# Sixteen of 22 contraction tiles of a last projection put through Strassen's method

## The chip, the cores and the metric

The kernel runs on one core of a Trainium2 chip. The metric is the device time of one execution in microseconds; the median of three runs of the kernel before is 2008.83 us (2007.9 to 2009.86). Times called "at 1873.53" are microseconds from the start of the profiled execution's span.

## The reference

Two layers of a streaming encoder on x of 1 x 512 x 1024 (float32). Each layer is a half-step SwiGLU FFN, a mixer (gated DeltaNet heads and a convolution module) and a second half-step FFN, each between two RMSNorms, then a block norm. The change touches only the last product of the second layer's second FFN and what follows it:

```python
def swiglu_ffn(x, w_in, w_out):        # D_MODEL 1024, D_FF 2816
    h = x @ w_in
    gate, up = h[..., :D_FF], h[..., D_FF:]
    return (jax.nn.silu(gate) * up) @ w_out
...
    h = swiglu_ffn(rms_norm(x, ffn2_norm_pre[l]), ffn2_w_in[l], ffn2_w_out[l])
    x = x + 0.5 * rms_norm(h, ffn2_norm_post[l])
    x = rms_norm(x, block_norm[l])
```

## The kernel before

Every large product is computed to nearly full float32 precision from three products of rounded float32r operands: high by high, high by low and low by high, where high is the rounded tensor (ScalarE, ACT, makes it) and low is the exact tensor minus high (VectorE, DVE, makes it). Weights come by DMA into four slots `raw` (512 KB each, the SP queue issues them), ACT writes `wh`, DVE writes `wl`, and TensorE (PE) takes both. Semaphores count the units: `lo_full` after each `wl`, `unit_done` when PE has used a slot.

An FFN computes 22 tiles (128 rows) of h. Tiles 5 to 20 (`CONV0`, `NS` = 16) already go through a seven-product Strassen scheme in the FFN's first product, one tile per `body`, on all three engines in software-pipelined order; the tiles 0 to 4 and 21 are plain pairs of `in_unit`. After the last `body`, PE runs `in_unit` for the gate half of tile 21, two remaining products (`p4`, `p3`) and `in_unit` for its up half. Meanwhile ACT (`h_high`, `h_rounded`) and DVE (`h_low`) split the 16 exact tiles `hraw` into `hh` and `hl`, two at a time; DVE also finishes the tiles 20 and 21 (lines 2406 to 2431).

For the last FFN of the last layer PE then runs `rows_out` (line 831). Here h is the stationary operand (128 contraction rows by 128 tokens) and the weights stream past in 512 columns, so the output has tokens on partitions. The output is 4 token chunks `c` by 2 column halves, and its eight 128x512 accumulators fill the eight PSUM banks (`row_banks`). For each of 22 contraction tiles k there are 4 chunks x 3 products x 2 halves = 24 matmuls (`row_tile`, line 816). The first 18 tiles go k by k over all chunks. The last four (`HELD`) stay in the four slots and are taken chunk by chunk, so that chunk 0 is complete first and its tail runs beside the matmuls of chunks 1 to 3.

The weights of a tile are one DMA of 512 KB (line 510), one ACT copy of 128x1024 (line 1356, `high`) and one DVE subtraction of 128x1024 (line 2074, `weight_low`), with four slots in flight. The two gain rows (`grow`) are loaded in the middle.

The tail of a chunk (lines 1973 to 2022 on ACT, 2817 to 2892 on DVE): ACT squares the two halves out of PSUM and sums them, DVE multiplies the same banks by the gain into `yrow` and adds the residual row (turned by PE's `turn_row` into the freed banks), ACT squares that, DVE scales it twice into `xin`, and SP stores it. The order of each engine is written out by hand: ACT `row_root(0)`, `row_root(1)`, `block_root(0)`, `row_root(2)`, `block_root(1)`, `last_square(0)`, `block_root(2)`, `last_square(1)`; DVE `row_gained`, `row_factor`, `row_added`, `row_scaled` likewise. An engine never passes a waiting instruction. `steps.link(x)` on DVE issues x and waits for its completion.

Of the kernel before, what the change touches and what calls it, by code (L numbers as in the profile page):

```python
# [46 lines left out]
def trunk_kernel(nc, x, ffn1_norm_pre, ffn1_w_in, ffn1_w_out, ffn1_norm_post, mix_norm_pre, mix_w_in,  # L47
# [103 lines left out]
    T2_, T3_, T1_, T4_ = range(4)  # L151
    ring = at("ring", [P, 2, SLOTS * 8 * P], F32, o_wh)
# [99 lines left out]
    with ctx:  # L252
# [89 lines left out]
        conv_hi, conv_lo, conv_done = [sem(n) for n in ("conv_hi", "conv_lo", "conv_done")]  # L342
        rows_done, R_DONE = s_xturn, KD
# [75 lines left out]

        HELD = 4  # L420
# [31 lines left out]
        def _(sp):  # L452
# [13 lines left out]
            for l in range(L):  # L466
                def ffn(f):
# [39 lines left out]
                    if f == 1 and l == L - 1:  # L507
                        for k in range(KF):
                            sp.wait_ge(lo_full, l * UNITS + UBASE[f] + IN_U + k + 1)
                            sp.dma_start(raw[:, k % SLOTS, :, :].rearrange("p a b -> p (a b)"),  # L510
                                         ffn2_w_out[l, k * P:(k + 1) * P, :]).then_inc(raw_full[k % SLOTS], 16)
                            if k == KF // 2:

                                sp.wait_ge(h_ready, L * NP)
# [31 lines left out]
            for c in range(NC):  # L546
                for half in range(2):
# [5 lines left out]
                    sp.dma_start(out[0, c * P:(c + 1) * P, cols], xin[:, c, cols]).then_inc(s_out, 16)  # L553
# [62 lines left out]
        def _(pe):  # L616
# [199 lines left out]
            def row_tile(c, k, halves=(0, 1)):  # L816
                tokens = slice(c * P, (c + 1) * P)
                for j, (h, w) in enumerate(((hh, wh), (hh, wl), (hl, wh))):
                    for half in halves:
                        mm = pe.matmul(row_banks(c)[:, half, :], h[:, k, tokens],  # L820
                                       w[:, k % SLOTS, 4 * half:4 * half + 4, :].rearrange("p a b -> p (a b)"),
                                       start=k == 0 and j == 0, stop=k == KF - 1 and j == 2)
                return mm
# [7 lines left out]
            def rows_out(u1):  # L831
                at0 = (L - 1) * UNITS + u1 + SLOTS
                pe.wait_ge(pair_free, (L - 1) * NP + 2 * KF - 1)
                pe.wait_ge(c12_out, 2 * L * NS + 2)
                for k in range(KF - HELD):
                    if k in range(CONV0, CONV0 + NS, 2):
                        pe.wait_ge(conv_done, (2 * L - 1) * NCONV + (k - CONV0) // 2 + 1)
                    pe.wait_ge(lo_full, at0 + k + 1)
                    pe.wait_ge(h_ready, (L - 1) * NP + KF + k + 1)
                    for c in range(NC):  # L840
                        if k == 0 and c >= 2:
                            pe.wait_ge(pair_free, (L - 1) * NP + 2 * KF - 3 + c)
                        mm = row_tile(c, k)
                    mm.then_inc(unit_done, 1)
                for c in range(NC - 1):
                    for k in range(KF - HELD, KF):
                        if c == 0 and k in range(CONV0, CONV0 + NS, 2):
                            pe.wait_ge(conv_done, (2 * L - 1) * NCONV + (k - CONV0) // 2 + 1)
                        if c == 0:
                            pe.wait_ge(lo_full, at0 + k + 1)  # L850
                            pe.wait_ge(h_ready, (L - 1) * NP + KF + k + 1)
                        mm = row_tile(c, k)
                    mm.then_inc(rows_done, 1)
                    if c in (1, 2):

                        pe.wait_ge(rows_sq, R_SQ + 2 * c)
                        pe.wait_ge(rows_gained, R_GAINED + 2 * c)
                        turn_row(c - 1, row_banks(c - 1))
                for half in range(2):
                    for k in range(KF - HELD, KF):  # L860
                        mm = row_tile(NC - 1, k, (half,))
                    mm.then_inc(rows_done, 1)
                    if half == 0:
                        pe.wait_ge(rows_sq, R_SQ + 2 * 3)
                        pe.wait_ge(rows_gained, R_GAINED + 2 * 3)
# [485 lines left out]
        def _(act):  # L1351
# [93 lines left out]
            def ffn(f, l):  # L1445
# [100 lines left out]
                def body(s, odd, first=False, final=False):  # L1546
# [16 lines left out]
                    if final:  # L1563
                        act.wait_ge(prod_done, st * PRODS + 7 * s + 6)
                        high(u0 + 2 * (KF - 1) + 1, 3, 8, l)
                        h_high(0)
                        h_high(1)
# [21 lines left out]
                def out_high(v):  # L1589
                    high(u0 + IN_U + v, v, 8 if last else part[v % 3], l)  # L1590
# [29 lines left out]
                body(NS - 1, 0, final=True)  # L1620
                h_rounded(0)
# [22 lines left out]
                if last:  # L1644
                    for k in range(SLOTS, KF):
                        high(u0 + IN_U + k, k % SLOTS, 8, l)
                    return
# [52 lines left out]
            for l in range(L):  # L1700
# [271 lines left out]
                ffn(1, l)  # L1972
            def row_root(c):
                act.wait_ge(rows_done, R_DONE + c + 1)
                for half in range(2):
                    if half:
                        act.wait_ge(rows_gained, R_GAINED + 2 * c + 1)
                    act.activation(spare[:, half * T:(half + 1) * T], row_banks(c)[:, half, :], ACT.Square,
                                   accum_out=yss[:, c, half:half + 1]).then_inc(rows_sq, 1)
# [12 lines left out]
            def last_square(half):  # L1992
                act.wait_ge(rows_done, R_DONE + NC + half)
                act.activation(spare[:, half * T:(half + 1) * T], row_banks(3)[:, half, :], ACT.Square,
                               accum_out=yss[:, 3, half:half + 1]).then_inc(rows_sq, 1)
# [26 lines left out]
            act.activation(xin[:, 3, T:D], xin[:, 3, T:D], ACT.Copy, scale=xrec[:, 3:4]).then_inc(row_out_last, 1)  # L2022
# [3 lines left out]
        def _(dve):  # L2026
# [186 lines left out]
            def ffn(f, l):  # L2213
# [116 lines left out]
                def body(s, odd, made=True, first=False, final=False):  # L2330
# [16 lines left out]
                    if final:  # L2347
                        weight_low(u0 + 2 * (KF - 1) + 1, 3, 8, l)
                        h_low(0)
                        h_low(1)  # L2350
# [9 lines left out]
                def out_low(v):  # L2360
                    weight_low(u0 + IN_U + v, v, 8 if last else part[v % 3], l)
# [44 lines left out]
                ps = pair_steps()  # L2406
                up_second(LAST_S, 0)
# [8 lines left out]
                p = KF - 1  # L2416
                dve.wait_ge(unit_done, l * UNITS + u0 + 2 * p + SLOTS + 1)
                dve.tensor_tensor(gs[:, 1, :], in_bank(unit_bank(6, stage, l)), rs[:], ALU.mult).then_inc(gate_scaled, 1)
                h_low(4)
                dve.wait_ge(unit_done, l * UNITS + u0 + 2 * p + SLOTS + 2)  # L2420
                dve.tensor_tensor(us[:, 1, :], in_bank(unit_bank(7, stage, l)), rs[:], ALU.mult).then_inc(pair_free, 1)
                dve.wait_ge(pair_free, l * NP + f * KF + p + 1)
                dve.wait_ge(silu_done, l * NP + f * KF + p + 1)
                ps.link(dve.tensor_tensor(hf[:], gs[:, 1, :], us[:, 1, :], ALU.mult))
                ps.link(dve.tensor_scalar(hh[:, p, :], hf[:], 1.0, None, ALU.mult))
                dve.tensor_tensor(hl[:, p, :], hf[:], hh[:, p, :].bitcast(F32), ALU.subtract).then_inc(h_ready, 1)
# [5 lines left out]
                if last:  # L2432
                    for k in range(SLOTS, KF):
                        weight_low(u0 + IN_U + k, k % SLOTS, 8, l)
                    return
# [380 lines left out]

            def row_gained(c):
                dve.wait_ge(rows_done, R_DONE + c + 1)
                for half in (1, 0):
                    if half == 0:  # L2820
                        dve.wait_ge(rows_sq, R_SQ + 2 * c + 1)
# [96 lines left out]
```

## Time and profile before

| | |
|---|---|
| median of 3 runs | 2008.83 us |
| profiled execution, first to last instruction | 2007.0 us |
| PE busy | 1958.0 us (98%), 12162 matmuls |
| DVE busy, ACT busy | 1440.1 us (72%), 1140.7 us (57%) |
| `rows_out` on PE | from 1873.53 to 1996.8 us, 528 matmuls of 128x512 |
| tail after the last matmul | to 2007.0 us |

The profiled execution lasts 2007.0 us by its span; the runs' median is 1.8 us more. Busy time counts the instructions of an engine; a matmul's end is modelled, so the time from one start to the next (the pitch) says more than the mean duration. A timeline row gives start, duration, engine, line, operation, output<-inputs, shape, and in brackets an idle time before it with what ended it. "x2" merges equal neighbours: their time runs from the first start to the last end.

### The profile page before, as it was taken

Reading aid. Unit: us, or ns where it says so; the run is one execution under the profiler, and the core shown is the slowest. Engines: PE = TensorE matmul, PEld = TensorE weight load, DVE = VectorE, ACT = ScalarE, POOL = GpSimd, SP = SyncE. Lnnn points to the kernel's source line nnn. Section 1 sums busy time; section 2 is a strip of 40 time slices with the busy share of each in tenths; the row PEclk is TensorE's granted clock in tenths of the full one; section 3 lists DMA queues with packets and bytes.
Section 4 is the critical chain, followed back from the end, with each engine's and each line's share of the span. In section 5 each row is a group of like instructions: output and inputs, shape, how many; then the busy total and the mean of one; then the engine's idle time right before and its main releaser. Section 6 shows DMA issues by size and latency. Waiting matters only on the chain.

```text
span 2007.0 us, 33275 instructions
## 1 busy us (share of the span) xinstructions
PE 1958.0 (98%) x12162; PEld 1751.0 (87%) x12162; DVE 1440.1 (72%) x2129; ACT 1140.7 (57%) x1915; POOL 149.2 (7%) x196
## 2 busy tenths in 40 slices
PE   9999999999999999999999999999999999999997
PEld 7899988878988799988878999888879887999886
DVE  5988832699785888872388888337997868888524
ACT  6566742457765566662365667325586655666623
POOL 1111000011000011100001110000110000111000
PEclk9999999999999999999999999999999999999999
DMA  6466533376222366643315664433761223666421
GB/s 174 104 156 156 145 106 100 79 163 139 61 53 84 84 146 151 157 125 99 98 53 127 157 157 130 116 101 77 171 147 27 64 74 90 161 156 149 158 95 42
DMA packets 351424, 232.49 MB, mean 116 GB/s; under 512 B 11123, under 2 KB 324949, under 8 KB 351317
## 3 DMA queue, kind: packets, MB, share of 16 engines
q1 hardware_dynamic: 327396, 177.55, 30.9%
q0 software_dynamic: 23904, 53.49, 14.9%
q8 instruction: 70, 1.15, 0.2%
q14 instruction: 38, 0.30, 0.0%
q10 hardware_dynamic: 16, 0.00, 0.0%
HBM read 175.43 MB, written 2.10 MB: 88 GB/s over the span
## 4 chain that ended last, share of the span: by engine, by line
PE 72%; DVE 16%; ACT 7%; issue 4%; DMA 1%; POOL 0%; SPq 0%; DVEq 0%; ACTq 0%
PE res L654 9%; PE res L655 9%; PE res L656 9%; PE res L889 7%; PE res L891 7%; PE res L892 7%; DVE u L2491 4%; PE sp L820 3%; PE sp L889 3%; PE sp L891 3%; PE sp L892 3%; PE res L820 2%; DVE cacc L2573 2%; PE sp L1132 1%; PE sp L1141 1%
## 5 line engine op out<-in xcount | busy, mean ns | idle before, releaser
L2074 DVE TENSOR_TENSOR wl<-raw,wh 128x1024 fp32r<-128x1024 f32 (+1 forms) x167 | 197.3, 1185 | 336.4 <-ACT wh L1356 335.9
L1356 ACT ACTIVATE wh<-raw 128x1024 fp32r<-128x1024 f32 (+1 forms) x205 | 209.7, 1029 | 332.0 <-PE res L656 238.0
L654 PE MATMUL res<-xh,wh 128*128 128x512 f32 x536 | 214.8, 401 | 10.7 <-DVE wl L2074 6.5
L889 PE MATMUL res<-xh,wh 128*128 128x256 f32 x768 | 218.6, 285 | 4.3 <-DMA wl<-raw 2.8
L891 PE MATMUL res<-xl,wh 128*128 128x256 f32 x768 | 217.7, 283 | 0.0
L892 PE MATMUL res<-xh,wl 128*128 128x256 f32 x768 | 217.6, 283 | 0.0
L656 PE MATMUL res<-xh,wl 128*128 128x512 f32 x536 | 210.0, 392 | 0.0
L655 PE MATMUL res<-xl,wh 128*128 128x512 f32 x536 | 209.7, 391 | 0.0
L656 PE MATMUL res<-hh,wl 128*128 128x512 f32 (+1 forms) x528 | 198.7, 376 | 0.0
L654 PE MATMUL res<-hh,wh 128*128 128x512 f32 (+1 forms) x528 | 198.7, 376 | 0.0
L655 PE MATMUL res<-hl,wh 128*128 128x512 f32 (+1 forms) x528 | 198.7, 376 | 0.0
L602 POOL DMA_DIRECT2D wl<-raw x128 | 108.9, 855 | 1012.2 <-ACT wl L1497 998.9
L2491 DVE SCALAR_TENSOR_TENSOR u<-glu,call,u 128x512 f32<-128x512 f32 x240 | 167.8, 746 | 0.3
L889 PEld LDWEIGHTS res<-xh,wh 128*128 128x128 f32 x768 | 147.5, 192 | 6.3 <-ACT wh L1507 3.1
L889 PE MATMUL res<-th,wh 128*128 128x256 f32 x512 | 145.7, 285 | 5.0 <-DVE wl L2277 2.6
L891 PEld LDWEIGHTS res<-xl,wh 128*128 128x128 f32 x768 | 147.5, 192 | 0.2
L892 PEld LDWEIGHTS res<-xh,wl 128*128 128x128 f32 x768 | 147.5, 192 | 0.0
L889 PE MATMUL sp<-th,wh 128*128 128x256 f32 x512 | 145.3, 284 | 1.8 <-DVE us L2300 1.8
L891 PE MATMUL sp<-tl,wh 128*128 128x256 f32 x512 | 145.2, 284 | 0.0
L892 PE MATMUL sp<-th,wl 128*128 128x256 f32 x512 | 145.1, 283 | 0.0
L891 PE MATMUL res<-tl,wh 128*128 128x256 f32 x512 | 145.1, 283 | 0.0
L892 PE MATMUL res<-th,wl 128*128 128x256 f32 x512 | 145.1, 283 | 0.0
(419 smaller groups left out, 4884.2 us busy)
## 6 DMA issues: line engine op xcount, KB each, us to landing
raw<-in_ffn_w_in SPq DMA_DIRECT2D x176, 512.0 KB, 4.1
wl<-raw POOLq DMA_DIRECT2D x128, 256.0 KB, 5.3
raw<-in_mix_w_in SPq DMA_DIRECT2D x48, 512.0 KB, 4.0
raw<-in_ffn_w_out SPq DMA_DIRECT2D x46, 512.0 KB, 4.0
raw<-in_ffn_w_out SPq DMA_DIRECT2D x48, 448.0 KB, 3.8
wl<-raw POOLq DMA_DIRECT2D x38, 512.0 KB, 5.0
raw<-in_mix_w_out SPq DMA_DIRECT2D x16, 512.0 KB, 4.2
xin<-in_x SPq DMA_DIRECT2D x8, 256.0 KB, 5.9
```

Of the source, the lines that this page charges most:

```text
L602: pool.dma_start(wl[:, 2, ks, :].bitcast(F32), raw[:, 2 * ((SP0 + s) % 2), ks, :], accum_op=ALU.add).then_inc(form_added[half], 16)
L654: pe.matmul(bank, wh[:, slot, j, :], hi, start=first, stop=False)
L655: pe.matmul(bank, wh[:, slot, j, :], lo, start=False, stop=False)
L656: return pe.matmul(bank, wl[:, slot, j, :], hi, start=False, stop=last)
L820: mm = pe.matmul(row_banks(c)[:, half, :], h[:, k, tokens], w[:, k % SLOTS, 4 * half:4 * half + 4, :].rearrange("p a b -> p (a b)"), start ...
L889: pe.matmul(bank, wh[:, slot, j, :], hi[:, k, :], start=first and k == 0, stop=False, skip_group_check=True)
L891: pe.matmul(bank, wh[:, slot, j, :], lo[:, k, :], start=False, stop=False, skip_group_check=True)
L892: mm = pe.matmul(bank, wl[:, slot, j, :], hi[:, k, :], start=False, stop=k == 3, skip_group_check=True)
L1356: act.activation(wh[:, slot, 0:nk, :], raw[:, slot, 0:nk, :], ACT.Copy).then_inc(hi_full, 1)
L2074: dve.tensor_tensor(wl[:, slot, 0:nk, :], raw[:, slot, 0:nk, :], wh[:, slot, 0:nk, :].bitcast(F32), ALU.subtract).then_inc(lo_full, 1)
L2491: ins = dve.scalar_tensor_tensor(u[:, t, :], src, w, u[:, t, :], ALU.mult, ALU.add)
L2573: ins = dve.scalar_tensor_tensor(cacc[:, n % 2, :], pre[:, k:k + T], w, cacc[:, n % 2, :], ALU.mult, ALU.add)
```

## The change

The contraction tiles 5 to 20 are taken in eight pairs j: tile 5+j (`SUMMED`) and tile 13+j (`DIRECT`). With tokens halved (256 each) and output columns halved (512 each), each pair is a 2x2 block product, done by the seven-product form of Strassen's method. A product is 2 token chunks x 3 = 6 matmuls of 128x512. Four products per pair come in a first pass over j (S3*T3, S2*T2, S1*T1 and A11*B11), three in a second (A22, S4 and A12 with their weights), and the six plain tiles follow, the last four of them chunk by chunk as before. The banks c22, c21, c12 accumulate one product each over the first pass; these and c11 are then copied out (`alone`, eight ACT copies of 128x512), the second pass accumulates on in c21, c12 and c11, and six DVE additions (`make_addends`) make the three sums that each chunk's tail adds to its banks (`row_sum`).

Removed: `h_high`, `h_low`, `h_rounded` and the weight splits of this stage. The other three FFN outputs stay as they are. Operand work, first pass, per pair j: DVE forms S1, S2, S3, S4 (four subtractions or additions of 128x256), the weight sums (three of 128x512), the low parts of h (128x768 and 128x256) and of the weights (1024, 512, 512). ACT makes the matching high parts. Second pass, per pair: DVE one weight sum of 512, low parts 1024 and 512, and 512 and 256 of h. Weight slots are used in pairs, so two sets of operands are in flight. `h_last` is the finish of tile 21 (lines 2422 to 2426), `up_last` line 2421.

```diff
 # PE, rows_out (rows_product: 2 token chunks x 3 matmuls of 128x512)
-                for k in range(KF - HELD):
-                    ...
-                        mm = row_tile(c, k)
-                    mm.then_inc(unit_done, 1)
+                for j in range(NJ):
+                    q = j % 2
+                    pe.wait_ge(a_low, W0 + j + 1)
+                    pe.wait_ge(w_low, W0 + j + 1)
+                    mm7 = rows_product(j, q, F_S3, 4 + F_S3, 3, c22, j == 0)
+                    mm6 = rows_product(j, q, F_S2, 4 + F_S2, 2, c21, j == 0)
+                    if j == 0:
+                        pe.wait_ge(pair_free, (L - 1) * NP + 2 * KF)
+                    mm5 = rows_product(j, q, F_S1, 4 + F_S1, 0, c12, j == 0)
+                    ...
+                    rows_product(j, q, F_A11, 4 + F_A11, 1, c11, j == 0).then_inc(rows_unit, 1)
+                for j in range(NJ):
+                    ...
+                    rows_product(j, q, F_A22, 4 + F_A22, 2, c21)
+                    rows_product(j, q, F_S4, F_S4 + 1, 0, c12)
+                    rows_product(j, q, F_A12, 4 + F_A12, 1, c11).then_inc(rows_unit, 1)
+                n = len(PLAIN) - HELD
+                for i in range(n):
+                    pe.wait_ge(w_low, W0 + 2 * NJ + i + 1)
+                    ...
 # SP: 512 KB of the summed tile, 256 KB of the direct one, then 512 KB of the direct one again
+                                if j < 2:
+                                    sp.wait_ge(lo_full, l * UNITS + UBASE[f] + IN_U + 2 * j + n + 1)
+                                else:
+                                    sp.wait_ge(w_low, W0 + j - 1)
+                                load_row(2 * (j % 2) + n, k, cols)
 # ACT
+                def forms_high(j):
+                    act.wait_ge(a_sum, W0 + j + 1)
+                    act.activation(h_cells(j, 1, 3), h_cells(j, 5, 3, False), ACT.Copy)
+                    act.activation(h_cells(j, 0), hraw[:, SUMMED[j], SECOND_T], ACT.Copy).then_inc(a_high, 1)
+                def sums_high(j):
+                    ...
+                        act.wait_ge(rows_unit, W0 + j - 1)
+                    act.wait_ge(w_sum, W0 + j + 1)
+                    act.activation(w[:, 0:2 * T], r[:, 0:2 * T], ACT.Copy).then_inc(w_high, 1)
+                    act.activation(w[:, 3 * T:4 * T], r[:, 3 * T:4 * T], ACT.Copy).then_inc(w_high, 1)
+                    act.activation(w[:, 2 * T:3 * T], kept_sums[j][:], ACT.Copy).then_inc(w_high, 1)
 # DVE
+                def form_sums_of_h(j, steps):
+                    ...
+                    at_s1 = steps.done(dve.tensor_tensor(s1, a21, a22, ALU.add))
+                    dve.tensor_tensor(s3, a11, a21, ALU.subtract)
+                    steps.need(at_s1)
+                    steps.link(dve.tensor_tensor(s2, s1, a11, ALU.subtract))
+                    dve.tensor_tensor(a21, a12, s2, ALU.subtract).then_inc(a_sum, 1)
+                def weight_sums(j, steps):
+                    ...
+                    dve.tensor_tensor(t3, b22, b12, ALU.subtract)
+                    steps.link(dve.tensor_tensor(b12, b12, b11, ALU.subtract))
+                    dve.tensor_tensor(kept_sums[j][:], b22, b12, ALU.subtract).then_inc(w_sum, 1)
+                if last:
+                    up_second(LAST_S, 0)
+                    h_made(LAST_S - 1, 1)
+                    form_sums_of_h(1, ps)
+                    up_first(LAST_S, 0, ps)
+                    weight_sums(0, ps)
+                    forms_low(0)
+                    gate_times(LAST_S, 0)
+                    weights_low(0)
+                    forms_low(1)
+                    h_made(LAST_S, 0)
+                    form_sums_of_h(2, ps)
+                    form_sums_of_h(3, ps)
+                    gate_last()
+                    weight_sums(1, ps)
+                    forms_low(2)
+                    up_last()
+                    forms_low(3)
+                    weights_low(1)
+                    h_last()
+                    for j in range(2, NJ):
+                        if j + 2 < NJ:
+                            form_sums_of_h(j + 2, ps)
+                        weight_sums(j, ps)
+                        if j + 2 < NJ:
+                            forms_low(j + 2)
+                        weights_low(j)
+                        if j >= 6:
+                            later_forms_low(j - 6)
+                    ...
+                    for j in range(1, NJ):
+                        later_weight_sum(j)
+                        later_weights_low(j)
+                        if j + 1 < NJ:
+                            later_forms_low(j + 1)
+                    dve.wait_ge(a_low, W0 + 2 * NJ)
+                    make_addends(ps)
+                    for i in range(len(PLAIN)):
+                        plain_low(i)
+                    return
 # tail, DVE: row_sum before row_gain; chunks 0 and 1 sum both halves, 2 and 3 the first
+            def row_sum(c, half):
+                n = (0, 1)[half] if c < 2 else 2
+                dve.tensor_tensor(yrow[:, c, half * T:(half + 1) * T], row_banks(c)[:, half, :], addends[:, n, c % 2, :],
+                                  ALU.add).then_inc(row_summed, 1)
 # tail, ACT: the square of a summed half waits for row_sum
+            def row_square(c, half):
+                if c >= 2 and half == 1:
+                    src = row_banks(c)[:, half, :]
+                else:
+                    act.wait_ge(row_summed, W0 + (2 * c + half if c < 2 else c + 2) + 1)
```

## Rows read from the trace of the kernel before

**Rows 1.** Groups of instructions of the output stage, 1861 to 1997 us.

```profile
L820 PE MATMUL res<-wh,hh 128*128 128x512 f32 x88 | 28.1, 393 | 0.0
L2074 DVE TENSOR_TENSOR wl<-raw,wh 128x1024 fp32r<-128x1024 f32 x23 | 28.0, 1224 | 68.2 <-ACT wh L1356 68.2
L1356 ACT ACTIVATE wh<-raw 128x1024 fp32r<-128x1024 f32 x22 | 23.0, 1057 | 67.9 <-PE res L820 67.9
```

**Rows 2.** The chain that ended last, one of its steps (start, us, count).

```profile
1911.77 2.72 PE sp L820 x12
```

**Rows 3.** Timeline of DVE before and at the hand-over, 1843 to 1880 us.

```profile
1844.82 0.69 DVE L2267 TENSOR_TENSOR ring<-raw 128x512 f32<-128x512 f32 x1
1845.55 0.69 DVE L2268 TENSOR_TENSOR raw<-raw 128x512 f32<-128x512 f32 x1
...
1850.78 0.41 DVE L2300 TENSOR_TENSOR us<-us,res 128x256 f32<-128x256 f32 x1
1851.11 0.68 DVE L2328 TENSOR_TENSOR hraw<-gs,us 128x512 f32<-128x512 f32 x1
1851.71 0.69 DVE L2284 TENSOR_TENSOR wl<-raw,wh 128x512 fp32r<-128x512 f32 x1
...
1861.17 2.35 DVE L2357 TENSOR_TENSOR hl<-hraw,hl 128x1024 fp32r<-128x1024 f32 x2
...
1866.83 0.42 DVE L2313 TENSOR_TENSOR us<-us,sp 128x256 f32<-128x256 f32 x1 [1.13 <-PE sp L892]
1867.28 0.69 DVE L2317 TENSOR_TENSOR us<-us,rs 128x512 f32<-128x512 f32 x1
```

**Rows 4.** Timeline of ACT, the same stretch.

```profile
1843.13 0.62 ACT L1497 ACTIVATE wl<-raw 128x512 fp32r<-128x512 f32 x1
1843.65 0.62 ACT L1498 ACTIVATE wh<-raw 128x512 fp32r<-128x512 f32 x1
...
1859.53 2.00 ACT L1583 ACTIVATE hl<-hraw 128x1024 fp32r<-128x1024 f32 x2
...
1868.74 0.36 ACT L1544 ACTIVATE gs<-res 128x256 f32<-128x256 f32 x1
```

**Rows 5.** Timeline of PE at the end of the first product.

```profile
1873.31 0.39 PE L656 MATMUL res<-xh,wl 128*128 128x512 f32 x1
1873.53 0.62 PE L820 MATMUL sp<-wh,hh 128*128 128x512 f32 x2
```

**Rows 6.** DMA issues, 1850 to 1990 us: count, size, median us to landing.

```profile
raw<-in_ffn_w_out SPq DMA_DIRECT2D x22, 512.0 KB, 3.5
```

**Rows 7.** Timeline of the tail, 1976 to 2008 us.

```profile
1988.94 0.68 DVE L2825 TENSOR_TENSOR yrow<-res,grow 128x512 f32<-128x512 f32 x1
...
1995.26 1.28 DVE L2836 SCALAR_TENSOR_TENSOR xrow<-yrow,yrec,res 128x1024 f32<-128x1024 f32 x1
...
1996.63 1.06 ACT L1987 ACTIVATE spare<-xrow 128x1024 f32<-128x1024 f32 x1 [2.36 <-DVE xrow L2836]
...
2003.38 0.72 ACT L2022 ACTIVATE xin<-xin,xrec 128x512 f32<-128x512 f32 x1 [0.32 <-DVE xrec L2889]
```

**Rows 8.** Timeline of PE around its longest wait.

```profile
1050.58 0.39 PE L656 MATMUL res<-xh,wl 128*128 128x512 f32 x1
1054.08 0.47 PE L654 MATMUL res<-xh,wh 128*128 128x512 f32 x1 [3.12 <-DVE wl L2074]
...
1055.08 0.63 PE L654 MATMUL res<-xh,wh 128*128 128x512 f32 x1
1055.50 0.63 PE L655 MATMUL res<-xl,wh 128*128 128x512 f32 x1
...
1058.27 0.40 PE L656 MATMUL res<-xh,wl 128*128 128x512 f32 x1
```

**Rows 9.** Engine busy by stretch: length, PE, PEld, DVE, ACT, POOL, granted clock, DMA share, GB/s.

```profile
1056.00:1058.00 2.00, 2.00 (x6) 1.59 (x5) 2.00 (x3) 0.00 (x0) 0.00 (x0) 0.50 0.58 174
...
1873.53:1960.60 87.07, 87.07 (x386) 72.14 (x385) 27.82 (x26) 26.45 (x27) 0.00 (x0) 1.00 0.35 118
```

More of the change, by code:

```diff
@@ L1620, in ffn @@
                 body(NS - 1, 0, final=True)
+                if last:
+                    forms_high(1)
+                    gate_second(LAST_S, 0)
+                    sums_high(0)
+                    silu(KF - 2, 0)
+                    forms_high(2)
+                    forms_high(3)
+                    silu(KF - 1, 1)
+                    sums_high(1)
+                    act.activation(warm[:], eps[:], ACT.Sqrt)
+                    for j in range(2, NJ):
+                        if j + 2 < NJ:
+                            forms_high(j + 2)
+                        sums_high(j)
+                        if j >= 6:
+                            later_forms_high(j - 6)
+                    later_sums_high(0)
+                    for n in range(8):
+                        alone(n)
+                    for j in range(1, NJ):
+                        later_sums_high(j)
+                        if j + 1 < NJ:
+                            later_forms_high(j + 1)
+                    for i in range(len(PLAIN)):
+                        plain_high(i)
+                    return
                 h_rounded(0)
@@ L2348, in body @@
                         weight_low(u0 + 2 * (KF - 1) + 1, 3, 8, l)
-                        h_low(0)
-                        h_low(1)
+                        if last:
+                            form_sums_of_h(0, ps)
+                        else:
+                            h_low(0)
+                            h_low(1)
                     else:
@@ new lines, in plain_low, with make_addends @@
+                def plain_low(i):
+                    dve.wait_ge(w_high, W0 + 5 * NJ + i + 1)
+                    dve.tensor_tensor(wl[:, i % SLOTS], raw[:, i % SLOTS], wh[:, i % SLOTS].bitcast(F32),
+                                      ALU.subtract).then_inc(w_low, 1)
+                def make_addends(steps):
+                    dve.wait_ge(alone_out, W0 + 8)
+                    p7, p6, p5, p1 = [[h_cells(2 * n + t, 2, 2, False) for t in range(2)] for n in range(4)]
+                    for t in range(2):
+                        steps.link(dve.tensor_tensor(addends[:, 2, t, :], p1[t], p6[t], ALU.add))
+                        dve.tensor_tensor(addends[:, 1, t, :], p1[t], p7[t], ALU.add)
+                        steps.link(dve.tensor_tensor(addends[:, 0, t, :], addends[:, 2, t, :], p5[t], ALU.add))
@@ L2415, in ffn @@
                 h_made(LAST_S, 0)
-                p = KF - 1
-                dve.wait_ge(unit_done, l * UNITS + u0 + 2 * p + SLOTS + 1)
-                dve.tensor_tensor(gs[:, 1, :], in_bank(unit_bank(6, stage, l)), rs[:], ALU.mult).then_inc(gate_scaled, 1)
+                gate_last()
                 h_low(4)
[L2420 to L2426, printed above, removed]
+                up_last()
+                h_last()
                 out_low(2)
```

307 lines of the change are left out of this document (238 added, 69 removed).

## The prediction

> **What bounds the kernel now.** The page first: PE is busy 98% of the span, DVE 72%, ACT 57%, so in general a matmul saved is time saved. That average is of no use for one stage, so the second view is busy time by stretch. Over the first sixteen contraction tiles of the output PE is busy all 87.07 us at the full clock, DVE only 27.8 and ACT 26.5 [rows 9]. The groups of this stage agree: DVE's weight splits wait 68.2 us for ACT, whose copies wait 67.9 us for PE to free a slot, and PE waits for nothing [rows 1]. The chain of waits runs through PE in steps of twelve matmuls, 2.72 us each, a pitch of 0.2267 us [rows 2]. So PE sets the end here, and DVE has about 59 us to spare in 87. The question is what the change asks of DVE, and when.
>
> **Fewer matmuls.** Before: six groups of 88 like the first of [rows 1], 528. After: 8 pairs x 7 products x 6 = 336, and 6 plain tiles x 24 = 144, 480 in all, of the same shape and kind. 48 x 0.2267 = **10.9 us saved**. One pair is 24 matmuls = 5.44 us in the first pass, 18 = 4.08 us in the second; a plain tile is 5.44 us as before.
>
> **DVE's prices.** From start to next start [rows 3]: 128x512 0.60 us, 128x256 0.33, 128x1024 1.13 (2.35 less one duration of 1.22), and 768 between these, 0.86 (estimated from its neighbours). Where the instruction's own end is awaited: 512 0.73 (1844.82 to 1845.55), 256 0.45 (1866.83 to 1867.28). ACT [rows 4]: 1024 0.95, 512 0.52, 768 about 0.74, 256 about 0.3.
>
> **The first pass on DVE.** Sums of h 0.33 + 0.33 + 0.45 + 0.33 = 1.45; weight sums 0.60 + 0.73 + 0.60 = 1.93; low parts of h 0.86 + 0.33 = 1.20; low parts of weights 1.13 + 0.60 + 0.60 = 2.33. Together **6.9 us per pair, against PE's 5.44**. ACT needs 1.1 + 2.0 us per pair, in the shadow of DVE's next piece. So DVE is the bound of this pass for pairs 2 to 5, and PE idles 1.5 us per pair. Two operand sets in flight shift that, they don't remove it.
>
> **The hand-over**, followed in DVE's written order from 1861.2, where the first `h_low` starts now [rows 3]. Sums of pair 0 to 1862.6, `up_second` to 1863.0; ACT can make `forms_high(0)` only after the sums, which puts its silu behind them, to 1864.4, and `h_made` to 1864.5; sums of pair 1 to 1866.6; `up_first` waits for PE as now (1866.83) and ends 1868.0; weight sums 0 to 1869.9; low h 0 to 1871.1; `gate_times` 1871.7; low weights 0 done at 1874.1. PE wants them at 1873.5 [rows 5]: idle 0.6. Then come low h 1, `h_made`, sums 2 and 3, `gate_last`, weight sums 1, low h 2 and `up_last` (1.2 + 0.6 + 1.45 + 1.45 + 0.6 + 1.93 + 1.2 + 0.7 = 9.1), done at 1883.2. PE needs that `up_last` before its third product of pair 0, since c12 lies in the bank it reads: it arrives at 1874.2 + 12 x 0.2267 = 1876.9 and **waits 6.3 us**. Behind `up_last` on DVE stand low h 3 and low weights 1, done 1886.7 (PE idle 0.8), then `h_last` (0.73 + 0.47 + 0.6) and a full pair of 6.9: weights 2 done 1895.4 (PE idle 3.3). Pairs 3, 4 and 5 follow each 6.9 later (idle 3 x 1.5). Pairs 6 and 7 have no sums of h, but then nothing covers ACT's 1.05 us between weight sums and low weights: 5.4, and 6.3 for pair 7 with `later_forms_low(0)` (idle 0.1 and 1.0). The pass ends at 1933.7.
>
> **The second pass** costs DVE 0.60 + 1.13 + 0.60 + 0.60 + 0.33 = 3.3 us per pair and ACT 2.3, against 4.08 on PE. A slot pair freed by PE is filled again 2.9 us later (0.95 ACT, then 1.13 and 0.69 DVE), so PE stays busy but for 0.2. The copies `alone` (8 x 0.52 on ACT) are each ready before their bank's second product. `make_addends`, 4 linked x 0.73 + 2 x 0.60 = 4.1 us, stands before the first `plain_low`; the tile is ready 0.3 us late. Plain tiles cost DVE and ACT 2.1 us of 5.44, as now.
>
> Idle in all: 0.6 + 6.3 + 0.8 + 3.3 + 4.5 + 0.1 + 1.0 + 0.2 + 0.3 = **17.1 us against 10.9 saved, so PE ends 6.2 us later**.
>
> **The loads.** A pair brings 768 KB per 6.9 us = 114 GB/s, the stretch now runs at 118 [rows 9]. A load of 512 KB lands 3.5 us after its issue [rows 6]; those of pairs 2 to 5 are issued at least 8 us before use, those of pair 7 some 7 us before (issued 1916, wanted 1923). Nothing is added; one late landing there would cost 1 us.
>
> **The tail.** I followed the order of the three engines with the durations of [rows 7]; for the kernel before the same sums end at 2004.1, as the trace does (2003.38 + 0.72). `row_sum` reads a PSUM bank like the gain product does, 0.6 to 0.69 us [rows 7]. Two per chunk in chunks 0 and 1, one in 2 and 3. DVE's slack swallows part, and the residual add of chunk 2 (1995.26) comes 1.4 us later. Then ACT's `last_square(0)`, which before found its bank long ready, stands ahead of `block_root(2)` (1996.63) and waits for DVE's new `row_sum` of chunk 3: 0.6 + 0.6 more. All that follows to the last instruction moves: **+2.6 us**. Bounds: 0 if the queue hides it, 6 x 0.69 = 4.1 if nothing does.
>
> **Sum**: 2007.0 - 10.9 + 17.1 + 2.6 = 2015.8 us of span, 8.8 more. The runs' median is 1.8 above the span, so 2008.83 + 8.8 = **2017.6 us**, slower.
>
> **Bounds.** If DVE's fixed part per instruction vanished, a pair would still cost 5632 elements x 1.04 ns ((1224 - 690) / 512, [rows 1, 3]) = 5.9 us, about 1 us less on eight pairs: 2010. If starts don't overlap at all (0.41, 0.69, 0.96, 1.22 per form) it is 7.7, 0.8 more on eight: 2024. I take the pitches, since the timeline has each size but one.
>
> **The clock.** After PE's longest wait now, 3.12 us of idle time, matmuls go at a pitch of 0.42 us from 1055.08 and are back to 0.23 by 1058.27, granted 0.50 between [rows 8, 9]: the lower level, 1.2 GHz, for some 3 us. The wait of 6.3 us will do the same. Twelve matmuls of pair 0 at 0.42 cost up to 2.4 us, but pairs 1 and 2 are late by 0.8 and 3.3 anyhow, waiting for DVE; it disappears there. The Trainium skill ("TensorE: Matmul & The Clock Gate", section "HAM oscillation — how this bites in real kernels") says that waits between groups of matmuls can send the clock down before every group, not once. With 1.5 us of idle per pair the row leaves that open; it is the third rival.
>
> **Rivals.**
> 1. Hidden DVE work, the other side (faster). DVE has 59 us of idle time in the old stretch [rows 9]; if it ran far enough ahead, only the matmuls and the tail would count: 2008.8 - 10.9 + 2.6 = 2000.5. It decides if a pair costs DVE under 5.44 and `up_last` isn't behind the sums. Against it: raw slots and operand sets allow no more than two pairs ahead, h tiles exist only from 1861 on, and the work from there to pair 7 (66 us) exceeds what PE leaves (1861 to 1911.6 = 50).
> 2. Only the hand-over costs. If pairs ran at PE's pace after pair 1, idle is 7.8: 2008.8 - 10.9 + 7.8 + 2.6 = 2008.3, no change. It needs a pair at 5.4 on DVE, under the lower bound of 5.9.
> 3. The clock stays down in the first pass. 24 x 0.42 = 10.1 us per pair instead of 6.9 on some six pairs: +19, 2037. For it: a clock that falls in the long wait and then sees PE idle a fifth of the time. Against: recovery after 1055 was quick under a dense stream, and a few cold matmuls per pair (8 x 0.2 = 1.6 us) fit into the 1.5 us of idle.
>
> **Chances.** Forecast 0.82, rival 1 0.06, rival 2 0.06, rival 3 0.06. The range 2011 to 2025 takes in the bounds and a partly cold clock. About 0.2% (4 us) is what a measurement of this kernel tells from no change: faster 0.06, same 0.07, slower 0.87.
>
> **What would show it.** Right: PE waiting for DVE's sums and low parts in the first pass, about 17 us in ten waits; one wait of about 6 us in the third product of pair 0, on DVE's `us`; starts of pairs 2 to 5 some 6.9 apart with DVE full; the second pass at 4.1 per pair; a granted clock of 0.5 just after the long wait; 9.7 us from PE's last matmul (1997.0 now) to the end of the last ACT instruction, 7.1 now. Wrong: pairs less than 6 us apart, waits of PE on DMA in the first pass, or a clock at 0.5 over several pairs.

## The result: 0.45% slower, and the profile after

The changed kernel takes 2017.15 us (median of 4 runs, 2016.23 to 2017.8), the kernel before 2008.37 us on the same chip (4 runs). The ratio is 1.0045, 95% interval [1.0031, 1.0059]. Timed again beside the experiments it was 1.005 [1.0037, 1.0063]. The forecast was 2017.6 us, slower. Medians and ratios leave out three executions well above the rest (2060.73 and 4971.11 us of the kernel before, 5111.08 us of e8).

The page of the changed kernel, its head and the line of the granted clock; below the last dots, the loads of the stage (DMA issues, 1850 to 1990 us).

```profile
span 2015.1 us, 33375 instructions
...
PE 1950.2 (97%) x12114; PEld 1741.1 (86%) x12114; DVE 1501.4 (75%) x2253; ACT 1158.9 (58%) x1963; POOL 149.2 (7%) x196
...
PEclk9999999999999999999999999999999999999898
...
raw<-in_ffn_w_out SPq DMA_DIRECT2D x22, 512.0 KB, 3.9
raw<-in_ffn_w_out SPq DMA_DIRECT2D x8, 256.0 KB, 4.2
```

PE has less work and the span is longer; DVE has 61 us more work. By stretch (columns as in [rows 9]): the first pass, the second pass, and three pieces in which the clock was down for all or part of the time, one behind the long wait and two behind the next one.

```profile
1872.00:1932.56 60.56, 48.47 (x193) 38.07 (x193) 55.84 (x95) 30.11 (x48) 0.00 (x0) 0.92 0.37 119
1932.56:1965.80 33.24, 33.09 (x145) 26.76 (x143) 27.10 (x40) 19.12 (x30) 0.00 (x0) 1.00 0.37 121
...
1882.00:1884.00 2.00, 2.00 (x6) 1.53 (x5) 2.00 (x4) 1.32 (x2) 0.00 (x0) 0.50 0.00 0
...
1896.00:1898.00 2.00, 2.00 (x6) 1.52 (x6) 1.97 (x4) 1.16 (x3) 0.00 (x0) 0.50 0.70 274
1898.00:1900.00 2.00, 2.00 (x9) 1.59 (x8) 2.00 (x4) 1.37 (x3) 0.00 (x0) 0.80 0.00 0
```

In the first pass DVE is busy 55.84 of 60.56 us, in the same place where it was busy a third of the time [rows 9]; PE is the one with gaps. In the second pass PE is full again. What PE waits for in the whole stage (us in total, times, longest):

```profile
PE sp L860 <- DVE wl L2589: 6.2, 5, 2.3
PE res L860 <- DVE us L2674: 6.0, 1, 6.0
PE sp L869 <- DVE wl L2610: 0.2, 1, 0.2
```

Every listed wait is put down to DVE, none to a DMA or to ACT. The timeline of PE at the start of pair 0, at its third product, and at the starts of pairs 2, 4 and 5:

```profile
1872.51 0.47 PE L860 MATMUL sp<-wh,fa 128*128 128x512 f32 x1 [0.63 <-DVE wl L2589]
...
1881.49 0.79 PE L860 MATMUL res<-wh,fa 128*128 128x512 f32 x1 [5.99 <-DVE us L2674]
1882.08 0.63 PE L861 MATMUL res<-wl,fa 128*128 128x512 f32 x1
1882.51 0.63 PE L862 MATMUL res<-wh,fa 128*128 128x512 f32 x1
...
1893.92 0.47 PE L860 MATMUL sp<-wh,fa 128*128 128x512 f32 x1 [2.27 <-DVE wl L2589]
...
1907.95 0.47 PE L860 MATMUL sp<-wh,fb 128*128 128x512 f32 x1 [1.23 <-DVE wl L2589]
...
1914.96 0.47 PE L860 MATMUL sp<-wh,fb 128*128 128x512 f32 x1 [1.31 <-DVE wl L2589]
```

Single executions of the same code reach this stage at different times (PE was ready for pair 0 at 1871.88 here, at 1873.53 before, and between 1871.86 and 1877.0 in the changed-kernel variants below whose code up to there is the same). So I measure the stage from "PE ready" (start of the first matmul of pair 0 less its wait). Before: 123.43 us to the end of PE's last matmul (1996.96), then 7.14 to the end of ACT's last instruction, 130.57. After: 60.68 to the start of the second pass (1932.56), 69.77 to the end of the last matmul (2002.33), 9.85 of tail (2012.18), 140.30. The difference is **9.7 us**; the two ratios make it 9.0 and 10.0.

### The profile page after: what moved, and what is told of

The parts are those of the page before. It is cut to its first block, busy times and chain, and to the rows that moved or that the text cites. A ratio compares the mean times of both kernels' runs of the same rounds, so it can differ in the third digit from the quotient of the medians.

```text
span 2015.1 us, 33375 instructions
## 1 busy us (share of the span) xinstructions
PE 1950.2 (97%) x12114; PEld 1741.1 (86%) x12114; DVE 1501.4 (75%) x2253; ACT 1158.9 (58%) x1963; POOL 149.2 (7%) x196
## 4 chain that ended last, share of the span: by engine, by line
PE 68%; DVE 19%; ACT 7%; issue 4%; DMA 1%; POOL 0%; SPq 0%; DVEq 0%; ACTq 0%
PE res L688 9%; PE res L690 9%; PE res L689 9%; PE res L960 7%; PE res L963 7%; PE res L962 7%; DVE u L2798 4%; PE sp L960 3%; PE sp L963 3%; PE sp L962 3%; DVE cacc L2880 2%; PE sp L1203 1%; PE sp L1212 1%; ACT wh L1427 1%; DMA wl<-raw 1%
## 5 line engine op out<-in xcount | busy, mean ns | idle before, releaser
L2236 DVE TENSOR_TENSOR wl<-raw,wh 128x1024 fp32r<-128x1024 f32 (+1 forms) x145 | 170.5, 1179 | 269.1 <-ACT wh L1427 268.5
L1427 ACT ACTIVATE wh<-raw 128x1024 fp32r<-128x1024 f32 (+1 forms) x183 | 186.6, 1025 | 261.7 <-PE res L690 238.0
```

The source lines that it names most:

```text
L1427: act.activation(wh[:, slot, 0:nk, :], raw[:, slot, 0:nk, :], ACT.Copy).then_inc(hi_full, 1)
L2236: dve.tensor_tensor(wl[:, slot, 0:nk, :], raw[:, slot, 0:nk, :], wh[:, slot, 0:nk, :].bitcast(F32), ALU.subtract).then_inc(lo_full, 1)
```

## Experiments

The theory: DVE's 7.0 us per pair sets the pace of the first pass, DVE's queue up to `up_last` and the weights of pairs 1 and 2 sets the hand-over, and the tail adds 2.7. Rivals: PE's own work or a fallen clock sets the pace; or the time is lost elsewhere. All ratios are to the kernel before. "First pass" is from PE ready to the start of the second pass, in one trace. The ratios of single kernels are known to about 0.001 to 0.002 (2 to 4 us), so differences of 1 or 2 us are read from the traces only.

| kernel | ratio [95%] | first pass, us | starts of pairs 2 to 6 apart, us |
|---|---|---|---|
| changed | 1.0045 [1.0031, 1.0059] | 60.68 | 7.18 6.85 7.01 5.56 |
| changed, again | 1.0050 [1.0037, 1.0063] | 60.63 | 7.01 7.01 7.01 5.56 |
| e1_uplast_early | 1.0044 [1.0026, 1.0062] | 60.64 | 7.01 7.01 7.02 5.56 |
| e2_two_of_three | 1.0047 [1.0032, 1.0063] | 59.21 | 7.00 7.01 7.01 5.54 |
| e3_less_dve | 1.0020 [1.0008, 1.0032] | 55.51 | 6.01 6.02 6.01 5.56 |
| e4_pool_sums | 1.0062 [1.0041, 1.0082] | 63.50 | 5.55 5.57 5.54 5.95 |
| e5_row_sum_early | 1.0044 [1.0032, 1.0056] | 60.68 | 7.15 6.88 7.02 5.54 |
| e6_keep_warm | 1.0062 [1.0050, 1.0074] | 60.68 | 7.18 6.84 7.02 5.54 |
| e7_light_dve | 1.0007 [0.9998, 1.0016] | 51.79 | 5.44 5.44 5.44 5.44 |
| e8_six_more | 1.0063 [1.0050, 1.0076] | 60.88 | 7.01 7.02 7.01 6.92 |
| e9_eight_more | 1.0066 [1.0054, 1.0078] | 63.62 | 8.96 7.26 7.25 7.25 |

**The changed kernel again,** beside e5 to e7:

> The changed kernel as it stands, beside the three others on the same chip: 1.0045 of the kernel before, and a pass of eight pairs that ends 60 us after PE's first product.

Its first pass is 60.63 us against 60.68, its tail 9.86.

**e1: `up_last` early.**

```diff
                     h_made(LAST_S, 0)
+                    gate_last()
+                    up_last()
                     form_sums_of_h(2, ps)
                     form_sums_of_h(3, ps)
-                    gate_last()
                     weight_sums(1, ps)
                     forms_low(2)
-                    up_last()
```

> The changed kernel with gate_last and up_last ahead of the sums of h of pairs 2 and 3 in DVE's order, so that PE need not wait 6.0 us for the bank in pair 0. Same work. Theory (DVE is the bound of the first pass, and never idle from 1859 to the end of it): the idle time only moves, to before pair 1; pass one ends at the same time within 0.3 us and the whole stays at 1.0045 of the kernel before. Rival (the long wait and the cold clock behind it are a cost of their own): 6 us less, or up to 8 with the clock, a ratio near 1.001.

The wait in the third product is gone, and PE waits 6.6 us before pair 1 instead (the waits of e1's stage):

```profile
PE sp L860 <- DVE wl L2589: 13.4, 7, 6.6
PE sp L869 <- DVE wl L2610: 0.2, 1, 0.2
```

The first pass is unchanged at 60.64. The bank wait was never the cost: it was only the first place where PE noticed that DVE's queue is long.

**e2: a third of the first pass's matmuls left out.** The term low by high is missing in the four products of the first pass, 64 matmuls or 14.5 us of PE's work. Part of the computation is left out.

```diff
-                    pe.matmul(banks[t], hi, w_lo, start=False, stop=False, skip_group_check=True)
-                    mm = pe.matmul(banks[t], lo, w_hi, start=False, stop=True, skip_group_check=True)
+                    mm = pe.matmul(banks[t], hi, w_lo, start=False, stop=short, skip_group_check=True)
+                    if not short:
+                        mm = pe.matmul(banks[t], lo, w_hi, start=False, stop=True, skip_group_check=True)
```

> The first pass leaves out the third matmul of each product (low h by high weights): 64 matmuls of 128x512 fewer, 14.5 us of PE; part of the computation is missing. Theory: DVE sets the pace, so pairs 2 to 5 still start 7.0 us apart, PE only idles longer, and only the last pair's own length (5.44 to 3.63) comes off the time: 1.8 us less, ratio 1.0036. Rival (PE, its clock or its waits are the bound): up to 14.5 us less, ratio 0.997.

PE has 14.5 us less work. The first pass is 1.5 us shorter, all of it at its end, where the last pair is shorter, and the runs show no difference. PE's waits grow to 15.2 us in seven and one of 6.9. This is the strongest evidence against PE or its clock as the bound.

**e3: less work for DVE.** From pair 2 on, the low parts of two of the four weight blocks are made for 32 columns instead of 512; PE's work is the same, the other low columns hold older data, so part of the computation is left out.

```diff
+                    C = 32 if j >= 2 else T
-                    dve.tensor_tensor(w[:, 3 * T:4 * T], r[:, 3 * T:4 * T], high[:, 3 * T:4 * T], ALU.subtract)
+                    dve.tensor_tensor(w[:, 3 * T:3 * T + C], ...)
-                    dve.tensor_tensor(w[:, 2 * T:3 * T], kept_sums[j][:], high[:, 2 * T:3 * T],
+                    dve.tensor_tensor(w[:, 2 * T:2 * T + C], kept_sums[j][:, 0:C], ...)
```

> DVE's two low parts of 128x512 of the weight sums cover only 32 columns from pair 2 on (the rest of these low parts is left stale, so part of the computation is missing): 2 x 0.5 us less DVE work per pair in pairs 2 to 7. Theory: pairs 2 to 5 start 6.0 apart instead of 7.0 (4.0 us less), pair 6 is then held by PE (5.44), pair 7 too instead of 6.5 (1.0 less): 5.0 us less, ratio 1.002. Rival (PE's clock or the loads hold the pairs): no change.

One us less per pair on DVE makes the pairs start one us less apart. PE's timeline, pairs 3 to 5:

```profile
1904.04 0.47 PE L860 MATMUL sp<-wh,fa 128*128 128x512 f32 x1 [0.30 <-DVE wl L2591]
...
1910.06 0.47 PE L860 MATMUL sp<-wh,fb 128*128 128x512 f32 x1 [0.31 <-DVE wl L2591]
...
1916.07 0.47 PE L860 MATMUL sp<-wh,fb 128*128 128x512 f32 x1 [0.33 <-DVE wl L2591]
```

The first pass is 5.2 us shorter, and the ratio falls from 1.0045-1.0050 to 1.0020, by 5 to 6 us.

**e4: the sums of h on GpSimd,** an engine with no work in this stretch.

```diff
+            for j in range(NJ):
+                ...
+                at_s1 = pool_steps.done(pool.tensor_tensor(s1, a21, a22, ALU.add))
+                at_s3 = pool_steps.done(pool.tensor_tensor(s3, a11, a21, ALU.subtract))
+                ...
+                at_s2 = pool_steps.done(pool.tensor_tensor(s2, s1, a11, ALU.subtract))
+                ...
+                pool.tensor_tensor(a21, a12, s2, ALU.subtract).then_inc(a_sum, 1)
-                    form_sums_of_h(j + 2, ps)          # DVE, at its four places
```

> The four sums of h (128x256, two inputs in SBUF) of all eight pairs move from DVE to GpSimd, which is idle here. No row shows such an operation on GpSimd. If the engines work side by side and GpSimd needs less than 1.3 us per sum, DVE has 5.5 us per pair against 5.44 of PE, 8 x 1.45 = 11.6 us less up to pair 7: ratio 0.999. The rival: the two engines take turns, so DVE's instructions get longer while GpSimd works; with 0.6 to 0.9 us per sum that is 2.4 to 3.6 us per pair in the place of 1.45, ratio 1.008 to 1.013. The Trainium skill (SBUF — State Buffer) has this as a rule: an instruction of GpSimd that reads SBUF and one of VectorE with two SBUF inputs block one another.

The timeline of GpSimd (POOL) alone, while DVE waits for ACT, then of DVE and GpSimd while both work:

```profile
1865.89 0.74 POOL L662 TENSOR_TENSOR fa<-hraw 128x256 f32<-128x256 f32 x1
...
1885.14 0.67 DVE L2598 TENSOR_TENSOR raw<-raw 128x512 f32<-128x512 f32 x1
1885.17 1.24 POOL L665 TENSOR_TENSOR fb<-fb,hraw 128x256 f32<-128x256 f32 x1
...
1885.74 1.22 DVE L2599 TENSOR_TENSOR raw<-raw 128x512 f32<-128x512 f32 x1
1886.56 0.99 POOL L668 TENSOR_TENSOR hraw<-hraw,fb 128x256 f32<-128x256 f32 x1
...
1888.02 1.47 DVE L2570 TENSOR_TENSOR fa<-fa 128x768 fp32r<-128x768 f32 x1
...
1890.28 0.68 DVE L2696 TENSOR_TENSOR us<-res,rs 128x512 f32<-128x512 f32 x1
```

The 768 subtraction takes 1.47 us instead of 0.95, a 512 one 1.22 instead of 0.69: 0.52 to 0.53 us more each. Where DVE's started first (1885.14) it kept its 0.67, and GpSimd's took 1.24 instead of 0.74. `up_last`, which reads PSUM and an SBUF scale, keeps its 0.68. So the two engines take turns. That agrees with the Trainium skill ("SBUF — State Buffer", section "SBUF: two separate sides"): a DVE operation with two SBUF inputs and a GpSimd operation lock one shared port pair, and the later one waits for the whole of the other. GpSimd's sums run ahead and end at 1897, and from then on pairs cost DVE 5.55 us and start 5.5 apart. But in the hand-over both engines are slower: PE waits 5.5 us for pair 0, and the first pass is 2.8 us longer in all. What is gained later is lost before. The ratio, 1.0062, is neither of the two expected: the rival's mechanism is there, but only as long as GpSimd works.

**e5: the last `row_sum` early,** to test the tail.

```diff
             row_scaled(1, 2)
+            dve.wait_ge(rows_done, R_DONE + NC)
+            row_sum(3, 0)
             row_added(2, 3, row_banks(2))
             def last_gained(half):
                 if half == 0:
-                    dve.wait_ge(rows_done, R_DONE + NC)
-                    row_sum(3, 0)
```

> The changed kernel with row_sum of chunk 3 ahead of the residual add of chunk 2 in DVE's tail. Theory (ACT's square of chunk 3 waits for that sum and holds up block_root(2) behind it): block_root(2) starts 0.6 us earlier and from PE's last matmul to the end of the last ACT instruction it takes 9.3 us and not 9.85; in the whole 0.6 us less, which only the trace can show. Rival (the tail is longer by DVE's own added work, not by the order): the same 9.85 or more.

Timeline of e5, PE's last matmul and ACT's last instruction:

```profile
2004.55 0.39 PE L869 MATMUL res<-wh,hl 128*128 128x512 f32 x1
```

```profile
2013.39 0.72 ACT L2184 ACTIVATE xout<-xout,xrec 128x512 f32<-128x512 f32 x1 [0.32 <-DVE xrec L3219]
```

The tail is 9.17 us (2014.11 - 2004.94) instead of 9.85. The order of `row_sum` and the residual add is worth 0.7 of the 2.7 us; the runs alone cannot tell that. No experiment takes back the other 2.0.

**e6: 24 matmuls more in the long wait.** They repeat one operand pair into the bank that the fourth product later starts afresh.

```diff
                     if j == 0:
+                        for _ in range(24):
+                            pe.matmul(c11[0], h_cells(0, F_A11)[:, 0:P], flat_cell(wh, 0, 1), start=True, stop=True, ...)
                         pe.wait_ge(pair_free, (L - 1) * NP + 2 * KF)
```

> The changed kernel with 24 matmuls of 128x512 without use in PE's wait of 6.0 us in pair 0 (their bank is started afresh afterwards), 5.4 us of PE. Theory: the clock stays at 1.00 there, pair 0 ends some 2.4 us sooner, pair 1 waits longer for DVE, and the time is the same, ratio 1.0045. Rival (the fallen clock is part of the loss): 2 to 4 us less, 1.003.

PE's timeline at the third product, pair 1 and pair 2:

```profile
1883.07 0.50 PE L860 MATMUL res<-wh,fa 128*128 128x512 f32 x1 [0.54 <-DVE us L2677]
...
1886.70 0.47 PE L860 MATMUL sp<-wh,fa 128*128 128x512 f32 x1 [0.61 <-DVE wl L2592]
...
1895.51 0.47 PE L860 MATMUL sp<-wh,fa 128*128 128x512 f32 x1 [3.08 <-DVE wl L2592]
```

The clock stays at its upper level through the third product (granted 1.00 from 1882 to 1884, 0.50 in the changed kernel), and pair 2 still starts 21.42 us after pair 0, as in the changed kernel (21.41): the cold matmuls there cost nothing. The first pass is 60.68 in both. The runs are 2 to 3 us longer than the changed kernel's, with intervals that overlap. The stage doesn't account for that: from PE ready to ACT's last instruction it takes 140.30 us in both traces, and the 1.57 us by which the traced execution is longer (2018.42 against 2016.85) lie before PE was ready (1873.46 against 1871.88). Why the runs as a group are longer stays open.

**e7: a light DVE.** Two of the three weight sums are made for 32 of 512 columns in every pair, the low parts of weights for 32 columns per block from pair 2 on; `up_last` is early as in e1 and `h_last` comes after pair 3. PE's work is unchanged; part of the computation is left out.

```diff
+                    C = 32
-                    dve.tensor_tensor(t3, b22, b12, ALU.subtract)
+                    dve.tensor_tensor(t3[:, 0:C], b22[:, 0:C], b12[:, 0:C], ALU.subtract)
...
+                    C = 32 if j >= 2 else T
-                    dve.tensor_tensor(w[:, 0:2 * T], r[:, 0:2 * T], high[:, 0:2 * T], ALU.subtract)
+                    dve.tensor_tensor(w[:, 0:2 * C], r[:, 0:2 * C], high[:, 0:2 * C], ALU.subtract)
```

> Part of the computation is missing: from pair 2 on DVE's low parts of the weights cover 32 columns, two of the three weight sums cover 32 in all pairs; up_last comes early, and h_last after pair 3. DVE has some 3.8 us per pair left, under PE's 5.44. Theory: PE then idles only at the hand-over (about 3.6 us before pairs 0 and 1), the 48 matmuls saved show: 2008.4 - 10.9 + 3.6 + 2.7 = 2003.8, ratio 0.998, pairs from 2 on 5.44 apart. Rival (PE's small waits, the loads or the new form of matmuls cost the gain, not DVE): pairs still over 6 us apart and a ratio over 1.001.

The waits of e7's stage:

```profile
PE sp L860 <- DVE wl L2592: 5.7, 1, 5.7
PE sp L869 <- DVE wl L2613: 0.2, 1, 0.2
```

and its busy times by stretch, in pair 1 and over pairs 2 to 7:

```profile
1882.00:1884.00 2.00, 2.00 (x6) 1.54 (x5) 1.64 (x6) 1.33 (x3) 0.00 (x0) 0.50 0.85 255
...
1889.07:1921.71 32.64, 32.64 (x146) 27.03 (x145) 19.66 (x52) 18.97 (x31) 0.00 (x0) 1.00 0.45 153
```

From pair 2 on PE is full and pairs start 5.44 apart: the saving by matmuls is real. I expected 0.998; it is 1.0007. The wait before pair 1 was 5.7 us and not the 3.6 expected before pairs 0 and 1 together, and behind it the clock is down and makes pair 1 2.3 us longer (7.75). Here nothing absorbs that, since DVE is no longer late. Even so light, the first pass holds 8.3 us of idle and slow time; with 2.7 in the tail and 0.8 after the pass they outweigh the 10.9 saved.

**e8 and e9: more matmuls in pairs 2 to 5.** The term low by low of three products (e8, six matmuls a pair) or of four (e9, eight a pair).

```diff
-                    mm = pe.matmul(banks[t], lo, w_hi, start=False, stop=True, skip_group_check=True)
+                    mm = pe.matmul(banks[t], lo, w_hi, start=False, stop=not more, skip_group_check=True)
+                    if more:
+                        mm = pe.matmul(banks[t], lo, w_lo, start=False, stop=True, skip_group_check=True)
...
+                    mm7 = rows_product(j, q, F_S3, 4 + F_S3, 3, c22, j == 0, 2 <= j < 6)
```

> Pairs 2 to 5 of the first pass get six more matmuls each, the term low by low of the first three products (24 in all, 24 x 0.2267 = 5.44 us of PE's work). Theory (DVE sets the pace there, a pair costs it 7.0 us and PE has 5.44 + 6 x 0.2267 = 6.80 us to do): nothing is added to the time. Pairs 2 to 6 still start 7.0 us apart, PE's waits on DVE's wl in pairs 3 to 5 shrink from 1.2-1.5 us to under 0.3, and the ratio to the kernel before stays at 1.0045 to 1.005. Rival (PE's own work, or the clock that falls in PE's pauses, sets the pace): each pair is 1.36 us longer, pairs 2 to 6 start 8.4 us apart, 5.4 us more in all, ratio 1.0075.

> The same with the fourth product too: eight more matmuls in each of pairs 2 to 5, 5.44 + 8 x 0.2267 = 7.25 us of PE's work per pair against DVE's 7.0. Theory: the bound changes hands just here. Pairs 3 to 6 start 7.25 us apart without a wait, about 1 to 1.3 us more in all than in the changed kernel, ratio 1.005 to 1.0055. Rival: pairs 8.8 us apart, 7.3 us more in all, ratio 1.0085.

In e8's trace 5.44 us of matmuls cost 0.2: pairs start 7.01 apart as before, and its only waits in the first pass are those of the hand-over. PE waits of e8, then of e9:

```profile
PE res L860 <- DVE us L2676: 6.0, 1, 6.0
PE sp L860 <- DVE wl L2591: 2.8, 2, 2.2
```

```profile
PE res L860 <- DVE us L2676: 6.0, 1, 6.0
PE sp L860 <- DVE wl L2591: 3.2, 2, 2.6
```

In e9 the bound has changed hands: 7.25 apart, by PE's matmuls. It is 2.9 us longer than the changed kernel where I expected 1 to 1.3. The first step, from pair 2 to 3, is 8.96: the clock fell after the wait before pair 2, and since PE is now the bound its 1.7 us is paid. The first piece of e9's pair 2:

```profile
1896.00:1898.00 2.00, 2.00 (x6) 1.58 (x5) 1.97 (x5) 1.15 (x2) 0.00 (x0) 0.50 0.90 299
```

In e8's trace the clock stayed up there, behind a wait of 2.2 us:

```profile
1896.00:1898.00 2.00, 2.00 (x10) 1.63 (x9) 1.93 (x5) 1.15 (x2) 0.00 (x0) 1.00 0.95 290
```

The runs don't separate the two explanations: e8's 1.0063 lies above the 1.0045 to 1.005 that the theory gave and below the rival's 1.0075, and e9 is only 0.0003 more. The trace decides for the theory in the first pass, but it is a trace of e8's fastest execution (2018.29 us, mean granted clock 0.995). The four others took 2019.9 to 2021.3 us at 0.992 to 0.993. With 6.80 us of matmuls in 7.01, a pair of e8 has no room for slow ones, so a clock that falls before pair 2 as in e9 would be paid for there too, by an estimated 1.5 us (e9's 1.7 less the 0.2 of idle time). That may be part of the 3 us by which e8's runs exceed the changed kernel's; no trace shows it, and it stays open.

## Why the prediction was right

**PE's work saved, 10.9.** 48 matmuls fewer at a pitch of 0.2267; e7's pairs of 5.44 without a wait show that pitch throughout.

**PE's lost time, 17.1.** Measured: the first pass is 60.68 us for 192 matmuls (43.5), so 17.2 lost, and 0.75 after it (forecast 16.6 and 0.5). By place, forecast against trace: before pair 0, 0.6 and 0.63; third product of pair 0, 6.3 and 6.26; from there to pair 2, 0.8 + 3.3 = 4.1, and 1.83 of slow clock + 2.44 of idle = 4.27; pairs 3, 4, 5, 1.5 each, and 1.74, 1.41, 1.57; pair 6, 0.1 and 0.12; pair 7, 1.0 and 1.04. The split of the 4.1 was wrong in form: pair 1 didn't wait at all, the slow clock filled that time, as the paragraph on the clock said it would. The list has seven waits of 12.4 us in all, not ten of about 17: what the clock takes isn't listed as waiting, nor are the shortest gaps. e2 and e3 show that the cause is DVE: 14.5 us less work for PE don't matter, 1 us less per pair for DVE does.

**DVE's price per pair, 6.9.** It is 7.0. The timeline of one turn:

```profile
1893.70 0.42 DVE L2540 TENSOR_TENSOR fb<-hraw 128x256 f32<-128x256 f32 x1
...
1895.16 0.69 DVE L2576 TENSOR_TENSOR raw<-raw 128x512 f32<-128x512 f32 x1
...
1897.09 0.95 DVE L2548 TENSOR_TENSOR fb<-fb 128x768 fp32r<-128x768 f32 x1
1897.96 0.42 DVE L2550 TENSOR_TENSOR fb<-hraw,fb 128x256 fp32r<-128x256 f32 x1
1898.36 1.23 DVE L2585 TENSOR_TENSOR wl<-raw,wh 128x1024 fp32r<-128x1024 f32 x1
...
1900.70 0.42 DVE L2540 TENSOR_TENSOR fb<-hraw 128x256 f32<-128x256 f32 x1
```

1.46 + 1.93 + 1.27 + 2.34: the estimated 768 pitch (0.86) is 0.87, and only the step to the 1024 subtraction is 0.07 more than counted. Taking starts and not durations from [rows 3] decided this: by durations it would be 7.7.

**The hand-over.** `up_last` was to end 9.7 us after PE was ready; it ended 9.56 after. One sentence of that step is wrong: c12 doesn't lie in the bank that `up_last` reads. By the code one of c12's two banks is the one that `gate_last` reads, and `up_last` reads the second of c11's, which PE wants only nine matmuls later. The wait stands one product earlier than it needs to. It made no difference to the sum, because weights 1 come 3.5 us of DVE's work behind it anyhow, which e1 shows.

**The tail, 2.6.** It is 2.7 (9.85 against 7.14; forecast 9.7). ACT's wait for the last `row_sum`, and what stands before and behind it:

```profile
2002.05 1.28 DVE L3164 SCALAR_TENSOR_TENSOR xrow<-xrow,yrec,res 128x1024 f32<-128x1024 f32 x1
2003.24 0.68 DVE L3127 TENSOR_TENSOR yrow<-res,addends 128x512 f32<-128x512 f32 x1
2003.96 0.63 ACT L2134 ACTIVATE spare<-yrow 128x512 f32<-128x512 f32 x1 [3.47 <-DVE yrow L3127]
...
2004.71 1.06 ACT L2149 ACTIVATE spare<-xrow 128x1024 f32<-128x1024 f32 x1
```

`last_square(0)` (line 2134) waits for DVE and `block_root(2)` (line 2149) stands behind it, though its own operand was ready at 2003.3: the mechanism as forecast. Counted from PE's last matmul and against [rows 7], the residual add (line 3164) starts 1.42 us later than before (forecast 1.4) and `block_root(2)` 2.71 later, which is the whole 2.7. e5 takes back the part that the order costs.

**The sum.** By stage -10.9 + 17.2 + 0.75 + 2.7 = 9.7 where 8.8 was forecast: the saving was right, the tail 0.1 low and PE's lost time 0.8 low. The median came out 8.8 higher, in part by luck: the ratio of the second timing makes it 10.0. What moves the runs goes with the clock: the kernel before, timed beside the experiments, took 2004.9 us in the mean of six executions with a mean granted clock of 0.998 and 2010.6 in eleven with 0.995.

**The rivals.** Hidden DVE work did not happen: DVE was busy all but 4.7 us of the first pass and PE waited for it. It isn't only the hand-over that costs: the steady loss of about 1.5 per pair is there. The clock did not stay down: matmuls ran at the slow pitch twice, for 3 to 4 us each, and recovered inside a pair. The rule of the Trainium skill weighed there ("TensorE: Matmul & The Clock Gate", "HAM oscillation — how this bites in real kernels"), that waits between groups can send the clock down each time, does not reach to waits of 1.2 to 1.3 us, which are shorter than those of its own example: pairs 4 and 5 start 7.0 apart behind them, with no slow matmul. Behind the waits of 6.0 and 2.3 us the clock was down (0.50 in the pieces at 1882 and 1896).

**No version beats the kernel before.** e7, which leaves work out, shows what a lighter DVE alone brings: 1.0007, no difference from the kernel before. What it still loses is in the hand-over and the tail, but for 0.8 us. Whether plain tiles of weights, which cost DVE little, could fill PE's time in the hand-over was not tried. They share the accumulators with products that are copied out first, so this would need sums of its own.

## What to carry to other kernels

An algorithm that saves matmuls moves work to the engines that make operands: count both for the same unit (here a pair: 5.44 us of PE, 7.0 of DVE) and take DVE's price from start to start, not from durations. A stage average of a third busy says nothing if the new work must be done within one pass and can't be done ahead. And follow a wait back through the whole queue of the engine that ends it: removing the one wait that looks largest (6 us, e1) moved it and saved nothing.

## What was not expected of the hardware

- GpSimd is no free helper for DVE: in e4 a DVE subtraction of two SBUF operands that came second to a 128x256 GpSimd instruction took up to 0.53 us more, and one that read PSUM no more. GpSimd's own instruction took 0.74 us alone and 0.9 to 1.8 beside DVE.
- In these runs a slow clock cost time only where PE was the bound: 1.8 us in pair 0 of the changed kernel vanished (e6), 2.3 in e7 and 1.7 in e9 were paid in full.
- The clock isn't the same from run to run of one kernel: before pair 2 PE waited 2.3 us in the first execution of the changed kernel and the clock fell to 0.50 at 1896; in the second the wait was 1.1 us, behind a pair 1 that ended later, and it stayed at 1.00. In e8 it stayed at 1.00 behind a wait of 2.2. Both first passes of the changed kernel took 60.6 to 60.7 us.
